# First expert's bias products ahead of its row selection, and two smaller moves of work, in a fused decoder layer on one Trainium2 core

## The reference, cut to what matters

```
x      = x + gt1 * (merged @ w_o)                      # output projection, residual
h2     = rmsnorm(x, g_ffn) * (1 + sc2) + sh2           # sh2: the shift rows, one per request
logits = h2 @ w_router + b_router                      # 320 x 32
top-4 per token, softmax over the four -> gates
for each expert e:  X = rows of h2 that chose e
   gu  = X @ w_gate_up[e] + b_gate_up[e]               # 1024 -> 2048
   act = (clip(u) + 1) * g * sigmoid(1.702 g)
   out = act @ w_down[e] + b_down[e]                   # 1024 -> 1024
```

## Time and profile before

| what | value |
|---|---|
| median of 3 runs | 1382.12 us (1382.09 to 1383.41) |
| profiled execution | 1383.6 us, of which the span of instructions is 1381.8 us |
| PE busy | 1348.7 us (98%) |
| DVE, ACT, POOL busy | 499.6, 215.9, 69.0 us |
| DMA | 489.60 MB, mean 354 GB/s over the span |
| PE weight loads (overlapping) | 549.7 us |

### The profile page before, as it was taken

The page is one execution under the profiler, slowest core; times in us unless marked ns, Lnnn a source line. Parts: engine busy times, 40 slices in busy tenths (PEclk is TensorE's granted clock), DMA queues, the critical chain, the costliest instruction groups (busy, mean ns, idle before and its releaser), DMA issues.

```text
span 1381.8 us, 17459 instructions
## 1 busy us (share of the span) xinstructions
PE 1348.7 (98%) x6726; PEld 549.7 (40%) x6726; DVE 499.6 (36%) x1081; ACT 215.9 (16%) x402; POOL 69.0 (5%) x69
## 2 busy tenths in 40 slices
PE   8999999999999999999999999999999999999996
PEld 4544555555456333333333333333333333333332
DVE  3245886863124203333233222332223222233225
ACT  2111232221012111111111111111111111111102
POOL 1003402220002000000000000000000000000000
PEclk9999999999999999999999999999999999999998
DMA  9424354387879999999999999999999999999994
GB/s 386 162 102 167 122 122 164 105 285 283 352 288 398 402 401 418 421 424 423 429 426 429 428 429 428 429 427 430 427 429 429 428 429 428 430 427 430 427 427 180
DMA packets 63020, 489.60 MB, mean 354 GB/s; under 512 B 8459, under 2 KB 30539, under 8 KB 34548
## 3 DMA queue, kind: packets, MB, share of 16 engines
q1 hardware_dynamic: 60660, 484.15, 85.5%
q0 software_dynamic: 1152, 4.19, 0.8%
q10 hardware_dynamic: 1152, 0.52, 0.1%
HBM read 484.65 MB, written 4.15 MB: 354 GB/s over the span
## 4 chain that ended last, share of the span: by engine, by line
PE 81%; DMA 14%; DVE 3%; ACT 1%; issue 0%; SPq 0%; DVEq 0%
PE ps L1779 26%; PE ps L1807 14%; DMA ring<-in_w_gate_up 12%; PE ps L1106 6%; PE ps L1107 5%; PE ps L1697 5%; PE ps L1751 3%; PE ps L1121 3%; PE ps L1578 2%; PE ps L1765 2%; PE ps L1084 2%; PE ps L1755 1%; PE ps L1431 1%; PE ps L1792 1%; PE ps L1420 1%; DMA ring<-in_w_mid 1%
## 5 line engine op out<-in xcount | busy, mean ns | idle before, releaser
L1779 PE MATMUL ps<-ring,z 128*64 128x512 f32 x1536 | 340.2, 594 | 6.9 <-DMA ring<-in_w_gate_up 6.2
L2496 DVE TENSOR_SCALAR actT<-ps 128x512 f32<-128x512 f32 x32 | 22.1, 692 | 575.0 <-PE ps L1779 575.0
L1779 PEld LDWEIGHTS ps<-ring,z 128*64 128x64 f32 x1536 | 107.6, 137 | 233.5 <-issue 217.4
L1807 PE MATMUL ps<-ring,z 128*64 128x512 f32 x768 | 171.1, 594 | 0.2 <-ACT z L977 0.2
L1106 PE MATMUL ps<-ring,actT 128*128 128x512 f32 (+1 forms) x200 | 102.4, 594 | 1.3 <-DVE actT L1982 1.1
L1107 PE MATMUL ps<-ring,actT 128*128 128x512 f32 (+1 forms) x200 | 100.3, 583 | 0.0
L1807 PEld LDWEIGHTS ps<-ring,z 128*64 128x64 f32 x768 | 53.8, 137 | 111.6 <-issue 108.5
L1697 PE MATMUL ps<-z,actT 128*64 128x512 f32 x384 | 88.6, 596 | 1.1 <-DVE actT L2411 1.1
L1751 PE MATMUL ps<-z,aT 128*128 128x512 f32 x120 | 62.0, 619 | 0.0
L2442 DVE TENSOR_TENSOR xr<-xr,z 128x512 f32<-128x512 f32 (+1 forms) x75 | 59.8, 797 | 2.6
L1779 PE MATMUL ps<-z 128*64 128x512 f32 x260 | 59.1, 595 | 0.0
(11 more groups left out here) (367 smaller groups left out, 1296.1 us busy)
## 6 DMA issues: line engine op xcount, KB each, us to landing
ring<-in_w_gate_up SPq DMA_DIRECT2D x96, 2048.0 KB, 22.6
ring<-in_w_down SPq DMA_DIRECT2D x48, 2048.0 KB, 26.7
z<-in_w_gate_up SPq DMA_DIRECT2D x16, 2048.0 KB, 25.2
more_w<-in_w_gate_up SPq DMA_DIRECT2D x15, 2048.0 KB, 23.3
ring<-in_w_in SPq DMA_DIRECT2D x11, 2048.0 KB, 7.9
more_w<-in_w_down SPq DMA_DIRECT2D x9, 2048.0 KB, 32.3
ring<-in_w_mid SPq DMA_DIRECT2D x8, 2048.0 KB, 9.8
z<-in_w_down SPq DMA_DIRECT2D x7, 2048.0 KB, 23.6
```

The source lines that it names most:

```text
L1779: done = nc.tensor.matmul(bank(q // 2)[64 * (q % 2):64 * (q % 2) + 64, :], lhs, homes[home][4 * (k % 2) + q], start=False, stop=k == 7)
L1807: done = nc.tensor.matmul(bank(2)[64 * q:64 * q + 64, :], lhs, homes[home][2 * (k % 4) + q], start=k == 0, stop=k == 7)
```

## The change

Four edits. The two shift products, and DVE's readings of them, come one output tile later. `ebuf` for the first expert is written ahead of the first block of h2 on DVE, and no longer between `pick` and the third block. For the first expert `gate_up_bias`, and with it the wait for `late_here` 64, comes ahead of `x_rows`. The third block of h2 is signalled by halves, and the two products of `x_rows` on it wait for one half each.

```diff
             for c in range(KT):
                 out_tile(c)
-                if c == 0:
+                if c == 1:
                     shift_logits()
-                if c == 1:
+                if c == 2:
                     spread_shift_logits()
...
                     if n_zero and t == 2:
                         pe.wait_ge(h2s_done, 1)
                     for i in range(2):
+                        if n_zero and t == 2 and i:
+                            pe.wait_ge(h2s_done, 2)
...
             def experts(count, base):
-                x_rows(base, base == 0)
                 if base == 0:
                     pe.wait_ge(late_here, 64)
-                gate_up_bias(base, True)
+                    gate_up_bias(base, True)
+                x_rows(base, base == 0)
+                if base:
+                    gate_up_bias(base, True)
                 x_transpose(base)
...
                 x1_tile(c)
-                if c == 0:
+                if c == 1:
                     dve.wait_ge(tb_mm, 3)
                     nc.vector.tensor_copy(l2c[0:1 + DB], bank(2)[0:1 + DB, 0:NE]).then_inc(col_done, 1)
-                if c == 1:
+                if c == 2:
                     dve.wait_ge(tb_mm, 4)
...
             nc.vector.tensor_scalar(sel_m[:, 0:3, :], lrep, -2.0e38, None, ALU.is_lt).then_inc(selm_done, 1)
+            nc.vector.tensor_copy(ebuf, const("rowsel")[:, 0:1].broadcast_to([P, CAP])).then_inc(ebuf_done, 1)
             dve.wait_ge(sh2_here, 16 * (DB + 4))
...
             pick(0, pos_r, 0, True)
-            pick_bias(0, const("rowsel"), 0, True)
             nc.vector.tensor_scalar(nmr, m8r[:, :, 0], -1.0, None, ALU.mult).then_inc(m0_done, 1)
             dve.wait_ge(rows_tr, 15)
             for i in range(2):
                 h = slice(i * BANK, (i + 1) * BANK)
-                last = nc.vector.scalar_tensor_tensor(h2[0:NS, 2, h], bank(4)[i * NS:i * NS + NS], st[0:NS, 13:14], sh2s[0:NS, h],
-                                                      ALU.mult, ALU.add)
-            last.then_inc(h2s_done, 1)
+                nc.vector.scalar_tensor_tensor(h2[0:NS, 2, h], bank(4)[i * NS:i * NS + NS], st[0:NS, 13:14], sh2s[0:NS, h],
+                                               ALU.mult, ALU.add).then_inc(h2s_done, 1)
```

## The result

| | before | changed |
|---|---|---|
| median of 7 runs each, same chips | 1383.35 us (1382.09 to 1384.29) | 1387.56 us (1386.25 to 1387.94) |
| span of the profiled execution | 1381.8 us | 1385.6 us |
| mean granted clock in it | 0.997 | 0.994 |

The ratio is 1.0029 with a 95% interval of 1.0020 to 1.0039: slower by 4.0 us, 2.8 to 5.4. The forecast of 1383.9 us and its range, up to 1386.5, missed it on the fast side. Part of the distance is that before itself came to 1383.35 us with more runs, 1.2 us above the median known then; the rest is real, 4.2 us between the medians where 1.8 were forecast.

A forecast was written before the change was run, and what follows sets the result against it. The long expert stage was taken as held by PE and, late, by the weight stream; the first `gate_up` coming 1.8 us later put 1382.12 + 1.8 = 1383.9 us, range 1381.0 to 1386.5.

The forecast's parts named there:

- Edit 1: Shift products one output tile later: PE gains the 1.79 us wait for the router weight, ending the positions at 442.97.
- Edit 2: The `ebuf` copy earlier on DVE: 0.18 us, hidden by the position products with 0.12 us to spare, so no cost.
- Edit 3: First expert's bias products before row products: PE waits 4.2 us for the bias table, first `gate_up` 1.8 us later.
- The landing: Bias table's last packet by about 446.8 plus 0.4 us: PE starts the bias products at 447.2, bounds 447.0 to 447.6.
- The length of the row products: First expert's row products on PE: 2.58 us instead of 2.79, the 0.21 us being a wait for the third block.
- The clock: PE's clock in the new wait before the bias products: likeliest to stay full; a fall was given chance 0.17.
- rival B: PE's clock falls in the 4.2 us wait, products run at half rate: some 2.6 us more, 1386.5 us; chance 0.17.
- Edit 4: Third block of h2 signalled by halves: worth at most 0.21 us, and here nothing, as PE comes too late.
- The way to the end: Weight stream behind the first expert: a chunk issued 1.8 us later from an empty queue makes the end 1.8 us later.
- The likeliest case: First `gate_up` late by about 1.8 us at full clock: 1383.3 to 1384.6 us; chance 0.60.

The follow-up runs named there:

- table ahead: Changed kernel with the bias table's transfer issued ahead of one weight chunk instead of behind it: 1381.66 us, ratio to the kernel before 0.9994.
- 5 further products: Changed kernel with 5 added products on PE ahead of the bias-table wait, into a bank nobody reads: 1386.22 us, and 1386.08 us the second time.
- table ahead, either order: Changed kernel with the bias table issued before one chunk, bias products first (1381.66 us) or behind the row products (1381.49 us).
- the kernel before with the table ahead: Kernel before with only the bias table's transfer issued ahead of one weight chunk: 1383.74 us, ratio 1.0002.

## Why the prediction was wrong

- **Edit 1.** Right in place, and its 1.79 us in the profile of before was real. As the run with it alone shows, only 0.5 us of it reach the first `gate_up`, since the table holds PE there too; the prediction saw this wait only with edit 3.
- **Edit 2.** The cost on DVE was mis-sized: 0.72 us, not 0.18. The first block of h2 ended at 443.03, past the position products, not 0.12 us ahead of them. It cost nothing in the changed kernel, as the table's wait covered it; with the table ahead PE waited 0.40 us for that block.
- **Edit 3, the step that decides.** The mechanism was right: PE meets the wait at 442.7 instead of 448.7, behind a full queue. The landing was mis-sized. PE started at 447.85, not 447.2, 0.65 us later: the last small packets went by 0.4 us later in this execution (447.0:447.2), and the lag from there to PE's start was 0.65 us or more, not 0.4. The landing also moves more between executions than the bounds of 447.0 to 447.6 allowed: in the seven profiles in which PE waited for this table behind the same chunks it started at 447.34 to 448.42, and only one of them lies inside.
- **The length of the row products.** The sum put them at 2.58 us and took the 0.21 us above that for the wait for the third block. With PE coming as late as 449.12, long after that block was written, they still take 2.75 us at full clock. So the 0.21 us was no such wait. With the bias records at 1.09 behind a stop and the ACT moves and transposes 0.06 over the sum, the way from the bias products to `gate_up` is 5.95 us at full clock (5 further products: 454.05 - 448.10), not 5.65.
- **The clock: the step that failed.** The forecast took the wait at full clock as the likeliest and gave the fall of the clock (rival B) 17%. It came, in each of the three profiles with an unfilled wait of 4.7 to 5.2 us. I had compared the wait of 4.2 us with the one fall at the end of the kernel, 3.6 us after the work, and weighed it too low. In those three profiles it fell 1.6, 3.7 and 4.2 us after PE's last work. From the start of the bias products to `gate_up` the changed kernel took 7.48 us in the first profile, against 5.95 with the wait filled: the half clock cost 1.53 us there. In the other two it took 8.74 and 8.79, so 2.8. The sum of the first profile closes: 1.79 (forecast) + 0.65 (landing) + 0.30 (products and ACT at full clock) + 1.53 (clock) = 4.27 us. Filling the wait takes 3.0 us off on one chip, so the price of the clock is shown, not only argued. The runs with 5 further products also show that the forecast was low even at full clock: `gate_up` starts at 454.05 and 453.83 there, not 452.85, and the medians are 2.9 and 3.0 us above before, not 1.8. Rival B's difference to before, +4.4 us, is close to what was measured (+4.2), but in part by luck: its 2.6 us for the clock were 1.53 in the first profile, and the landing and the products made up for it.
- **Edit 4.** Worth nothing, as forecast. With the table ahead and the bias first it gave nothing either: the row records took 2.79 us, as before. Its "at most 0.21 us" was the misreading told above.
- **The way to the end.** Right: a chunk issued from an empty queue lands as much later as PE does, and 3.8 of 4.27 us reach the span. The other direction is less than one to one: 1.4 to 1.6 us at the first `gate_up` (table ahead, either order) gave 0.9 to 1.8 us in the median. What of that is the stream's own idle time and what is scatter these runs can't part.
- **The base.** The forecast was made upon 1382.12 us, the median of three; seven gave 1383.35. That alone put the upper end of the range 1.2 us too low; upon 1383.35 the range would have ended at 1387.7, just above the 1387.56 measured. The likeliest case would still have been 2.4 us under it.

## What to carry to other kernels

A wait that never shows in a profile may have little slack: before a consumer is moved ahead, find the landing of each transfer that it needs (its packets, what stands before it in the queue), and if it is late, move the small transfer ahead of a large one instead. Price a new stop of PE with its clock: 5 us of standing still were paid once as waiting and once more, with 1.5 to 2.8 us, as slow products after it. Where two orders of the same work each leave one hole of the same size, changing the order is worth nothing.

## What the runs showed of the hardware

**The clock also fell without the change.** In the profile of the kernel before with the table ahead, PE waits for the router weight as always, and then (timeline, then stretches):

```profile
403.62 0.63 PE L1601 MATMUL ps<-cT,mods 128*9 128x32 f32 x16 [1.85 <-DMA cT<-in_w_router]
```

```profile
400.00:404.00 4.00, 2.15 (x21) 1.35 (x20) 1.33 (x5) 0.47 (x1) 0.00 (x0) 1.00 1.12 292
404.00:408.00 4.00, 4.00 (x18) 2.73 (x14) 0.18 (x1) 0.00 (x0) 0.00 (x0) 0.65 0.96 295
408.00:412.00 4.00, 4.00 (x17) 2.67 (x16) 1.46 (x8) 0.47 (x1) 0.06 (x1) 0.93 1.05 446
```

A stop of 1.85 us was followed by 1.2 GHz with PE busy all the while; a stop of 1.79 us in the earlier trace rows was not. The tile behind it took 6.27 us instead of 4.57, and the row products began at 447.39 against 445.88, 1.5 us later. No other stop of PE stands in the 30 us before this fall, but no run took the stop away, so that it is the cause is argued, not shown. Such falls fit the scatter of the kernel before: of its 72 executions timed beside the experiments, the 5 with a mean granted clock of 0.995 took 1384.3 to 1385.3 us, 1384.9 on average, and the 67 with 0.996 to 0.998 took 1382.8 on average. Where the clock fell in those 5 no profile shows. The Trainium skill, page "TensorE: Matmul & The Clock Gate", section "HAM oscillation — how this bites in real kernels", sees the danger in idle gaps longer than this one; the trace shows a fall behind a shorter one.

**A copy on DVE stretched beside POOL.** 0.72 to 0.73 us next to POOL's additions (four in 2.78 us, 0.70 each), 0.18 to 0.19 elsewhere. DVE's `scalar_tensor_tensor` right behind it, reading PSUM, ran beside the same additions in 1.27 us, as before (1.28). The Trainium skill, page "SBUF — State Buffer", section "SBUF: two separate sides", says that DVE and GpSimd share one pair of ports, which only some DVE instructions need, and that whoever has it holds it for a whole instruction; the trace agrees in that the copy alone was held, and by 0.54 us, less than one addition of POOL. Which engine held the ports no view shows.
